# Squares added on Vector, and rotated rows exchanged by transfers

## The reference

```
rq = rotary(rq, pos); rk = rotary(rk, pos) * (RET_DK ** -0.5)      # retention: x1,x2 = halves of 64
#   rotary: concat(x1*cos - x2*sin, x2*cos + x1*sin)
q = rms_norm((h @ xq).reshape(B, S, 4, 256), xq_gain)              # cross-attention queries
q = _rmsnorm(cq, g_q) @ w_uq                                       # MLA: rank 768 = 6 tiles of 128
q_rope = _axial_rope(q[..., 64:96])                                # pairs of 8 columns change places
```

## Time and profile before

| | before |
|---|---|
| runs, us | 2397.44, 2401.75, 2402.91 (median 2401.75) |
| the profiled execution, us | 2397.45 |
| its span, first to last instruction, us | 2395.5 |
| TensorE busy | 2325.3 us, 97% |
| Vector, Scalar, GpSimd busy | 912.2, 874.8, 1102.9 us |
| TensorE's granted clock, mean | 0.995 of full speed |

### The profile page before, as it was taken

How to read it: one execution, slowest core, us unless ns; L and a number is a source line. 1 busy time by engine, 2 the same in 40 slices (tenths; PEclk the granted TensorE clock), 3 DMA queues, 4 the chain that set the end, 5 groups by cost and what they waited for, 6 DMA issues and landing times.

```text
span 2395.5 us, 33550 instructions
## 1 busy us (share of the span) xinstructions
PE 2325.3 (97%) x12124; PEld 1891.2 (79%) x12124; DVE 912.2 (38%) x1561; ACT 874.8 (37%) x1240; POOL 1102.9 (46%) x1356
## 2 busy tenths in 40 slices
PE   7999999899999999999999999999999999999997
PEld 6778687588888888888888888877766787888886
DVE  3324532498877771110111045234126554111113
ACT  3354543444233453212211234255434534422222
POOL 3333455099877764333333334333332054555544
PEclk9999999999999999999999999999999999999999
DMA  4222132256555531111211122222221022222222
GB/s 155 92 76 85 53 123 81 95 181 200 189 193 186 193 124 62 62 62 62 70 62 62 62 80 69 71 93 69 79 81 48 1 97 67 98 91 97 97 97 97
DMA packets 66604, 231.37 MB, mean 97 GB/s; under 512 B 7216, under 2 KB 9520, under 8 KB 66352
## 3 DMA queue, kind: packets, MB, share of 16 engines
q1 hardware_dynamic: 50656, 180.02, 21.9%
q10 hardware_dynamic: 15824, 49.55, 6.1%
HBM read 226.66 MB, written 2.10 MB: 95 GB/s over the span
## 4 chain that ended last, share of the span: by engine, by line
PE 60%; POOL 20%; issue 17%; DVE 2%; ACT 0%; POOLq 0%; DVEq 0%; ACTq 0%
PE ps L1783 46%; POOL WLO L343 20%; PE ps L2317 4%; PE ps L1818 1%; PE ps L2431 1%; PE ps L2444 1%; PE ps L2259 1%; PE ps L2288 1%; PE ps L2302 1%; PE ps L2432 1%; PE ps L2274 0%; PE ps L1804 0%; PE ps L1800 0%; PE ps L1799 0%; PE ps L2403 0%
## 5 line engine op out<-in xcount | busy, mean ns | idle before, releaser
L343 POOL TENSOR_TENSOR WLO<-RAW,WHI 128x256 fp32r<-128x256 f32 x1340 | 1087.5, 844 | 1248.7 <-ACT WHI L378 1248.0
L1783 PE MATMUL ps<-HLO,WHI 128*128 128x512 f32 (+2 forms) x1840 | 612.6, 367 | 5.7 <-DVE Y L1519 2.1
L1783 PE MATMUL ps<-HHI,WLO 128*128 128x512 f32 (+2 forms) x1840 | 605.3, 363 | 0.0
L1783 PE MATMUL ps<-HHI,WHI 128*128 128x512 f32 (+2 forms) x1840 | 604.2, 362 | 0.0
L378 ACT ACTIVATE WHI<-RAW 128x1024 fp32r<-128x1024 f32 x335 | 354.4, 1059 | 663.0 <-DMA RAW<-in_stream_dram 655.3
L1783 PEld LDWEIGHTS ps<-HLO,WHI 128*128 128x128 f32 (+1 forms) x1840 | 318.7, 188 | 69.0 <-issue 4.6
L1783 PEld LDWEIGHTS ps<-HHI,WHI 128*128 128x128 f32 (+1 forms) x1840 | 317.8, 188 | 58.9 <-issue 3.6
L1783 PEld LDWEIGHTS ps<-HHI,WLO 128*128 128x128 f32 (+1 forms) x1840 | 318.3, 188 | 55.8
L1378 DVE TENSOR_TENSOR SF<-SF,ps 128x512 f32<-128x512 f32 (+1 forms) x66 | 51.2, 777 | 495.5 <-PE ps L1783 486.3
L1783 PE MATMUL ps<-GLO,WHI 128*128 128x512 f32 (+1 forms) x704 | 231.6, 364 | 1.9 <-POOL WLO L343 1.9
L1783 PE MATMUL ps<-GHI,WLO 128*128 128x512 f32 (+1 forms) x704 | 231.5, 364 | 0.0
(11 more groups left out here) (373 smaller groups left out, 2887.9 us busy)
## 6 DMA issues: line engine op xcount, KB each, us to landing
RAW<-in_stream_dram SPq DMA_DIRECT2D x335, 512.0 KB, 3.2
ADA<-in_ada_dram ACTq DMA_DIRECT2D x72, 512.0 KB, 4.3
BM<-in_bias_dram ACTq DMA_DIRECT2D x8, 448.0 KB, 3.6
DECAY<-in_decay_dram ACTq DMA_DIRECT2D x4, 512.0 KB, 4.4
out_dram<-X SPq DMA_DIRECT2D x8, 256.0 KB, 2.2
X<-in_x_dram SPq DMA_DIRECT2D x2, 512.0 KB, 5.6
X<-in_x_dram ACTq DMA_DIRECT2D x2, 512.0 KB, 6.6
C<-in_mem_dram ACTq DMA_DIRECT2D x1, 1024.0 KB, 5.6
```

Of the source, the lines that this page charges most:

```text
L343: op = nc.gpsimd.tensor_tensor(WLO[:, slot(u), k:k + 2], RAW[:, slot(u), k:k + 2], WHI[:, slot(u), k:k + 2].bitcast(F32), ALU.subtract)
L1783: mm = nc.tensor.matmul(out, w, x[:, k, tok], start=(k == 0 and n == 0), stop=(k == kt - 1 and n == 2))
```

## The change

It does four things.

1. *Retention:* `ret_swap` on TensorE goes. After each copy Scalar waits for the copy and issues four transfers of 32 partitions each, `QF` to `QS` and `KF` to `KS`. Vector reads `QS` and `KS`.
2. *Cross-attention queries:* Vector adds the two squares of a head (`query_add`), and TensorE makes one sum for a head in place of two. The last sum of a turn is carried: it stands after the first unit or pair of the next turn, and the very last one after the first scores. The carrying applies to the retention-side `normed("dq")` too, whose number of sums stays.
3. *MLA rank norm:* Scalar squares and Vector adds six tiles, and TensorE makes one sum.
4. *MLA queries:* `turn_query` goes. Scalar issues four transfers of eight partitions for each head, after waiting for the copy and for the turn of head h-2. Heads 6 and 7 are turned inside the attention, at its steps 1 and 3.

```diff
+            def ret_swap(i, a):                       # Scalar
+                x, swapped = ((QF, QS), (KF, KS))[a]
+                act.wait_ge(s("ret_f"), 2 * i + a + 1)
+                if i:
+                    act.wait_ge(s("ret_r"), 6 * i)
+                for r in range(0, P, 32):
+                    act.dma_start(swapped[r:r + 32], x[r ^ 32:(r ^ 32) + 32]).then_inc(s(f"ret_swap{a}"), 16)
...
+                    act.wait_ge(s("ret_swap0"), 64 * i)
+                    act.wait_ge(s("ret_swap1"), 64 * i)
                 nc.scalar.activation(QF[:], ps[:, 5], ACT.Copy).then_inc(s("ret_f"), 1)
+                ret_swap(i, 0)
...
                 nc.scalar.activation(KF[:], ps[:, 6], ACT.Copy).then_inc(s("ret_f"), 1)
+                ret_swap(i, 1)
...
-                        act.wait_ge(s(tag + "_ms"), 4 * i + (j + 3))
+                        act.wait_ge(s(tag + "_ms"), g + (lane + 3))
...
-            norm2("cq", 6, [(lambda k: ps[:, CQ_BANKS[k]], 0, S)], S, 768, SQQ, RSQ, TNQ, lambda k: wait_unit(UNIT["cq"] + k), CQHI)
+            for k in range(6):
+                wait_unit(UNIT["cq"] + k)
+                square("cq", SQQ, k, k, [(ps[:, CQ_BANKS[k]], 0, S)])
+            norm2("cq", 6, [(None, 0, S)], S, 768, SQQ, RSQ, TNQ, None, CQHI)
...
                 nc.scalar.activation(q[0:QK_MLA, h % 4], ps[0:QK_MLA, UQ_BANKS[h % 4]], ACT.Copy).then_inc(s("mq_raw"), 1)
+                act.wait_ge(s("mq_raw"), h + 1)
+                if h >= 2:
+                    act.wait_ge(s("mq_rope"), 3 * (h - 2) + 3)
+                for r in range(64, QK_MLA, 8):
+                    act.dma_start(MQS[r:r + 8, h % 4], q[r ^ 8:(r ^ 8) + 8, h % 4]).then_inc(s(f"mq_swap{h % 2}"), 16)
...
-                V.tensor_tensor(TN[:, 1], ps[:, 3], SIN[:], ALU.mult).then_inc(s("ret_r"), 1)
+                dve.wait_ge(s("ret_swap0"), 64 * i + 64)
+                V.tensor_tensor(TN[:, 1], QS[:], SIN[:], ALU.mult).then_inc(s("ret_r"), 1)
...
+            def query_add(h):                         # Vector
+                dve.wait_ge(s("xq_sq"), 2 * h + 2)
+                V.tensor_tensor(SQ[:, 0], SQ[:, 0], SQ[:, 1], ALU.add).then_inc(s("xq_add"), 1)
...
+            query_add(0)
             for h in range(3):
                 query_scale(h)
+                query_add(h + 1)
...
-                    if n == 1:
-                        query_rope(7)
+                    if n in (1, 3):
+                        query_rope(6 + n // 2)
...
+            clear(ACCQ[:])
+            for k in range(6):
+                add_square("cq", ACCQ[:], SQQ, k, k)
...
                 ret_out(i)
-                ret_swap(i + 1)
                 ret_total(i, 1)
...
-                def turn(i):
+                def turn(i, carried=None):            # TensorE, normed
                     def total_of(j):
+                        if j % per < per - 1:
+                            return
...
                         if j:
                             total_of(j - 1)
+                        elif carried:
+                            carried()
+                    return lambda: total_of(3)
...
+                if n == 0:
+                    last_query()
...
-            sums2("cq", 6, S, SQQ)
+            pe.wait_ge(*norm_at("ckv", "ln", 1))
+            sum_of("cq", ACCQ[:], 6, tiles=6)
...
-                if h:
-                    turn_query(h - 1)
```

More of the change, by code:

```diff
@@ L166, in build @@
                                  ("SC", [P, 2, 1280], F32))
+        (QS, KS), _ = region(_, ("QS", [P, S], F32), ("KS", [P, S], F32))
         constr = put("constr", [P, 2, P], F32R, at=r2_at + 8 * S + 4 * (N2 + S))
@@ L213, in build @@
         (MQB,), _ = region(c_at, ("MQB", [P, 4, S], F32))
+        (MQS,), _ = region(q_at + 4 * S * 15 + 2048, ("MQS", [P, 4, S], F32))
         (MOHI, MOLO, MP, MPT), _ = region(q_at - 6144, ("MOHI", [P, 4, S], F32R), ("MOLO", [P, 4, S], F32R),
@@ L525, in turn @@
                         wait_unit(u0 + j, i)
-                        act.wait_ge(s(tag + "_ms"), 4 * i + (j + 1))
+                        act.wait_ge(s(tag + "_ms"), 4 * i + (j + 1) if per == 1 else 2 * i + (j // 2 + 2))
                         nc.scalar.activation(sq[:, j % 2, 0:n], ps[:, j, 0:n], ACT.Square).then_inc(s(tag + "_sq"), 1)
@@ L1733, in query_rope @@
             def query_rope(h):
-                dve.wait_ge(s("mq_swap"), h + 1)
-                rope("mq_rope", (MQA if h < 4 else MQB)[:, h % 4], 4 + h % 4, COSQ, SINQ, 3 * h)
-            for h in range(7):
+                dve.wait_ge(s(f"mq_swap{h % 2}"), 64 * (h // 2) + 64)
+                rope("mq_rope", (MQA if h < 4 else MQB)[:, h % 4], MQS[:, h % 4], COSQ, SINQ, 3 * h)
+            for h in range(6):
                 query_rope(h)
@@ L1843, in spin, with sum_of @@
                     nc.tensor.matmul(ps[:, bank, 0:P], const[:, ONES], const[:, IDENT], start=True, stop=True)
-            def sum_of(tag, acc, bank=7, wait=0, idle=0):
+            def sum_of(tag, acc, bank=7, wait=0, idle=0, tiles=KD):
                 spin(idle, wait)
-                pe.wait_ge(*norm_at(tag, "acc", KD + 1))
+                pe.wait_ge(*norm_at(tag, "acc", tiles + 1))
                 width = acc.shape[-1]
@@ L1921, in normed @@
             def normed(tag, u0, iters, per, n, ones, sq, x, x_tokens, ready=None, after=None, held=False):
-                def turn(i):
+                def turn(i, carried=None):
                     def total_of(j):
-                        pe.wait_ge(s(tag + "_sq"), 4 * i + (j + 1))
-                        nc.tensor.matmul(ps[:, 4 + (j // per) % 2, 0:n], ones, sq[:, j % 2, 0:n], start=(j % per == 0),
-                                         stop=(j % per == per - 1)).then_inc(s(tag + "_ms"), 1)
+                        if j % per < per - 1:
+                            return
+                        pe.wait_ge(*(s(tag + "_sq"), 4 * i + (j + 1)) if per == 1 else (s(tag + "_add"), 2 * i + j // 2 + 1))
+                        nc.tensor.matmul(ps[:, 4 + (j // per) % 2, 0:n], ones, sq[:, j % 2 if per == 1 else 0, 0:n], start=True,
+                                         stop=True).then_inc(s(tag + "_ms"), 1)
                     for j in range(4):
@@ L1939, in turn @@
                             total_of(j - 1)
-                    if i < iters - 1 or not held:
-                        total_of(3)
-                    else:
-                        return lambda: total_of(3)
+                        elif carried:
+                            carried()
+                    return lambda: total_of(3)
+                rest = None
                 for i in range(iters):
-                    rest = turn(i)
-                return rest
+                    rest = turn(i, rest)
+                if held:
+                    return rest
+                rest()
             def project(tag, u0, x, first):
@@ L2099, in _ @@
             pe.wait_ge(s("w_out_x"), KD + 4)
-            normed("xq", UNIT["xq"], 2, 2, S, const[:, ONES], SQ, (HHI, HLO), x_tok, ready=lambda k: (norm_at("n2", "hi", k + 1), norm_at("n2", "lo", k + 1)),
-                   after=lambda j: (key_total(3), pe.wait_ge(s("xk_q"), 3)) if j == 0 else pe.wait_ge(s("xk_q"), 4) if j == 2 else None)
+            last_query = normed("xq", UNIT["xq"], 2, 2, S, const[:, ONES], SQ, (HHI, HLO), x_tok, ready=lambda k: (norm_at("n2", "hi", k + 1), norm_at("n2", "lo", k + 1)),
+                   after=lambda j: (key_total(3), pe.wait_ge(s("xk_q"), 3)) if j == 0 else pe.wait_ge(s("xk_q"), 4) if j == 2 else None, held=True)
             pe.wait_ge(s("xq_q"), 7)
@@ L2425, in mla_scores @@
                 if n == 1:
-                    turn_query(7)
+                    pe.wait_ge(s("mq_raw"), 8)
                 if g == 0:
```

33 lines of the change are left out of this document (10 added, 23 removed).

## The result

| | median of the runs, us | ratio to before, with 95% interval |
|---|---|---|
| before (measured beside it) | 2399.99 | |
| changed kernel | 2412.48 | 1.0065 [1.0054, 1.0077] |

The changed kernel is slower by 12.5 to 15.6 us (difference of the medians, and the ratio times 2400). The forecast was 2403.9 us and no change, its range ended at 2410, and the nearest rival (the clock falls at each new idle time) said 2409.9. TensorE has 25 products less, and the span is longer all the same. Two single executions of later experiments (3308 us of "late issues", 9360 us of "issues from Sync") lie far off and count in neither ratio.

The account below looks back on a forecast made before the run. It took the waits around TensorE's edits, not its 97% busy share, to decide. Terms -0.4 + 1.3 - 0.7 - 0.5 + 1.7 + 0.8 = +2.2 us on 2401.75 gave 2403.9, called no change; range 2394 to 2410.

Parts of the forecast that it names:

- the clock falls at each new idle time: Rival, chance 0.27: lower clock behind new idle times in retention (3 x 1.7) and MLA queries (0.8); +8.1 us, 2409.9.
- retention: Retention stage: first two permutations save 1.7 us, three later sums cost 1.3; together -0.4 us.
- cross-attention queries, with clock: Cross-attention queries: +1.3 us for the order, TensorE idle 2.9 us ahead of unit 6, and +1.7 for the clock.
- rank norm, with clock: MLA rank norm: adds at 0.74 us each, root 0.9 to 0.2 earlier, taken as -0.7 us; +0.8 for the clock.
- MLA queries: MLA queries: Scalar's period of 5.1, then 3.9 us; first exponential 2.1 earlier, 1.6 lost at an extra turn; -0.5 us.
- What bounds the kernel: Whole kernel: three of four edits remove products TensorE ran while it would wait anyway, or lengthen its next wait.
- Retention, the price of an issue: Scalar's list in retention: 0.57 us an issue, 0.34 for DECAY; sum 0.4 us late, three times, +1.3.
- Retention, the clock: Retention's new idle times of 2.2 us, three times: no fall of the clock charged.
- Retention, the first two permutations: Pair 0, between two value units whose weights are ready: 2 x 0.86 = 1.7 us saved.
- Landing hidden: Retention's swapped rows: some 9 us until the scores read them, so even a landing of 4.3 us is hidden.
- Cheap issues: Rival, chance 0.18: issues cost 0.34 us in retention and MLA queries; -6.8 us, 2395.0, faster.
- all 21.5 us saved: Rival, chance 0.05: TensorE's work is all that counts, so all 25 removed products are won; 2380.

Follow-up runs that it names:

- late issues: Changed kernel with retention's four KS<-KF issues of pairs 1 to 3 moved behind the copy and square of the output; 2402.42 us, ratio 1.0026.
- issues from Sync: Changed kernel with all exchange transfers of retention and the MLA queries issued from Sync's list, none from Scalar's; 2393.52 us, ratio 0.9981.
- part alone: Kernel before with only one part of the change: retention 1.0025, cross-attention queries 1.0020, rank norm 1.0007, MLA queries 1.0009.
- spins: Changed kernel with dummy TensorE products, which nobody reads, in the new idle times, no wait taken away; 2403.09 us, ratio 1.0027.
- squares in PSUM: Kernel before with only the rank norm's part, Scalar writing the squares to two free PSUM banks in place of SBUF; 2400.69 us, ratio 1.0005.
- two parts from Sync: Kernel before with only the retention and MLA queries parts, their transfers issued from Sync's list; 2391.93 us, ratio 0.9966.
- dummy products in the old idle times: Two parts from Sync plus fewer cross-attention sums, each placed inside the next unit; to that, dummy products added in three idle times; 2382.67 us, ratio 0.9937.

## Why the prediction was wrong

| step | forecast | part alone, by ratio | by its trace |
|---|---|---|---|
| retention | -0.4 | +6.0 | +7.8 |
| cross-attention queries, with clock | +1.3 +1.7 | +4.8 | +5.3 |
| rank norm, with clock | -0.7 +0.8 | +1.7 | +2.5 |
| MLA queries | -0.5 | +2.2 | +2.7 |
| sum | +2.2 | +14.6 | +18.3 |

- *What bounds the kernel.* Right: the products taken away stood where TensorE waits, and the waits around them decide.
- *Retention, the price of an issue.* Mis-sized: 0.61 us in the median with one of 0.59 for DECAY, where 0.57 and 0.34 were taken. The sum was 0.88 late, not 0.43. The term should have been 3 x 0.9 = +2.7 rather than +1.3. The upper bound (0.60) was the right end; I took a value nearer to it than to the lower one, but below it, because the smallest such issue was 0.52. Half of the miss is DECAY's, and it isn't its kind that costs: right behind the four KS issues it takes 0.59, and 0.34 to 0.38 where it stands alone, as before and in "late issues" (below). That an issue right behind another costs more stood in the trace of before: its first DECAY issue, right behind one for the memory, took 0.60.
- *Retention, the clock.* This is the step that failed. The forecast put the clock in retention at nothing: that it would not fall behind new idle times of about 2.2 us was the choice between the forecast and its first rival. The idle times came out at 2.65 to 2.8 us and the clock fell behind all three: 3 x 1.7, and once more at 34 us. The spins took back some 9 us over all stages and moved no wait. The rival's own condition, an issue price of 0.5 us or more, was met by the value that I used for the forecast, so the two were not independent cases: by my own sum the idle time was 2.2, and a price one step higher made it longer. The Trainium skill (TensorE: Matmul & The Clock Gate, part 1), by which the array is throttled unless activity releases it, spoke for that rival, and the traces agree at each of these places.
- *Retention, the first two permutations.* The 1.7 us are freed, but about 1.5 go to the clock at 34 to 38 us, behind the idle time of 2.35 us that before has too. It fell there in the profiles of all five kernels with retention's issues in Scalar's list, and in one of the eight others that have this idle time. Whether the issues do it, or the idle time lies at an edge and it is chance, is open.
- *Landing hidden.* Right: 2.0 to 3.3 us for KS (one of QS took 7.1, in the first pair), and no score waited for it.
- *Cross-attention queries.* Right in mechanism and place: 2.93 us idle at unit 6, clock 0.57 behind it. Too small in both terms. The order costs 2.3 us and not 1.3 (the spins' trace, where the clock does not fall in the stage): the first head's sum waits up to 1.40 us, since its add is behind a rounding that waited for weights, where I had Vector free at 384.42. The clock costs 1.4 us where it falls once (issues from Sync) and 2.3 to 3.0 where it falls twice, as in the changed kernel and in the part alone.
- *Rank norm.* Wrong in sign. I took 0.69 and a handoff for an add; they take 0.93 in the median and up to 1.03 beside GpSimd's subtractions, a tile then needs up to 1.13 us, and the passage is 2 us longer instead of 0.7 shorter. The median of 0.82 and the 1.245 stood in the earlier trace rows, but by the median my own sum still ended 0.2 earlier. With adds of 0.69 the passage is still 1.1 us longer (squares in PSUM): the sum itself is at the lower clock, 2.05 us where the spins make it 1.12, and that was not in the chain.
- *MLA queries.* Scalar's period decides, as forecast; its size was off: 5.55 and 4.3 us in place of 5.1 and 3.9, since four issues take 2.67 us and not 2.28. Over seven heads that is 3.1 us, and turns -2.1 at the first exponential into +1.1. The 1.6 us for the extra turn came out by luck. From the first exponential to the last it is 86.2 us before, 88.1 in the changed kernel and 87.8 in the part alone, which looks like it. But four kernels have the same extra turn and no fall of the clock there (spins, issues from Sync, two parts from Sync, dummy products in the old idle times), and they take 86.0 to 86.4; the five with the turn and a fall there take 87.2 to 88.1. The turn costs nothing that can be seen; what costs is the lower clock behind the idle time of 2.7 us, which the forecast put at nothing here too.
- *Cheap issues* (0.34 us) and *all 21.5 us saved* are out. Issues of 0.59 us or more that are in nobody's way won some 5 us against before with all four parts, and 8 with two.

## What to carry to other kernels

Price an issue by its own kind of transfer and by whether another stands right ahead of it, and ask whose list it stands in: with the same 64 issues, retention and the MLA queries lost 8 to 10 us against before from Scalar's list and won 8 from Sync's, whose list waits for the same events anyway. A new idle time of TensorE costs its own length and often 1.5 to 1.7 us of lower clock behind it; forecast the two together, and fill the time or move the sum inside the next unit. Over the fourteen profiles, from 20 us on, the clock fell behind all 23 idle times of 2.6 us or more and behind 24 of the 36 of 2.0 to 2.4 us. That is no threshold: behind the one of 1.91 us at some 455 us, which all fourteen have, it fell in eight. Give Vector's adds in SBUF 1.0 us where GpSimd works beside them.

## What was unexpected of the hardware

- Vector's adds and products on 512 columns with both operands in SBUF take 0.68 to 0.69 us alone (all 33 in the changed kernel) and, in most cases, 0.9 to 1.2 us beside GpSimd's subtractions. Two equal ones in the changed kernel; GpSimd subtracts from 1812.19 to 1816.38, all through the first, and again from 1817.74, when the second has 0.3 us left:

```profile
1813.41 1.22 DVE L1750 TENSOR_TENSOR MQA<-MQA,COSQ 32x512 f32<-32x512 f32 x1
...
1817.34 0.68 DVE L1750 TENSOR_TENSOR MQA<-MQA,COSQ 32x512 f32<-32x512 f32 x1
```

  With one operand in PSUM they take 0.69 under the same work (the squares in PSUM). That GpSimd is the cause is shown by where the long ones lie, not by taking it away.
- An issue right behind another costs more than the same issue alone. DECAY's on Scalar's queue, of the changed kernel, where all four stand right behind another, and of "late issues", where only the first does:

```profile
L491 ACTq DMA_DIRECT2D DECAY<-in_decay_dram x4: 592/595/600, 28.7 to 131.2; - x4
```
```profile
L492 ACTq DMA_DIRECT2D DECAY<-in_decay_dram x4: 335/360/598, 28.4 to 121.6; - x4
```

  For KS it is 0.51 us for the first of four and 0.61 in the median for the others.
- Eight partitions cost more to issue than 32 of the same row length, on Scalar's queue of the changed kernel:

```profile
L471 ACTq DMA_DIRECT2D KS<-KF x16: 514/612/686, 38.7 to 130.6; - x16
```
```profile
L1028 ACTq DMA_DIRECT2D MQS<-MQB x16: 631/632/662, 1823.8 to 1838.6; - x16
```

- A stretch of the feed-forward layer has two lengths, 201.1 and 205.0 us, at a granted clock of 1.00 in both. Its cause is open.
